# Hybrid decoder trunk on one core: the matmul queue's pair loop put at the start of a 16 KB piece of its program, two constant waits moved to their use, and the rotary keys' unit made fourth of the latent units

## The reference, cut to what matters

```python
def hybrid_layer(x, ...):
    h = rms_norm(x, norm_g)
    z = h @ w_in                     # 1024 x 9920, cut into eleven parts
    (x_rnn, g_rnn, sc_b, sc_c, x_sc, g_sc, c_q, c_kv, k_rope, g_att, gate_logits) = split(z)
    y_rnn = (rg_lru(x_rnn, ...) * silu(g_rnn)) @ rg_out
    y_sc  = (sc_b * depthwise(sc_c * x_sc) * silu(g_sc)) @ sc_out
    y_att = (mla(c_q, c_kv, k_rope, ...) * silu(g_att)) @ mla_out
    gates = sigmoid(gate_logits + gate_b)
    return x + (gates[0] * y_rnn + gates[1] * y_sc + gates[2] * y_att) @ w_out

def mla(c_q, c_kv, k_rope, ...):     # c_q 384 wide, c_kv 256, k_rope 64
    q = (rms_norm(c_q) @ w_uq)       # 8 heads of 128 + 64
    k = concat(rms_norm(c_kv) @ w_uk, k_rope for every head); v = rms_norm(c_kv) @ w_uv
    q, k = rms_norm(q), rms_norm(k); the last 64 of each are rotated by position
    return softmax(q k^T / sqrt(192), causal) @ v
```

## Time and profile before

| | us |
|---|---|
| median of 3 runs | 1804.34 (1803.9 to 1805.08) |
| the profiled execution's own time | 1801.34 |
| its span | 1799.5 |
| PE busy | 1742.7 (97%) |
| POOL, DVE, ACT busy | 1184.6, 807.1, 469.6 |

### The profile page before, as it was taken

How to read it: one execution, slowest core, us unless ns; L and a number is a source line. 1 busy time by engine, 2 the same in 40 slices (tenths; PEclk the granted TensorE clock), 3 DMA queues, 4 the chain that set the end, 5 groups by cost and what they waited for, 6 DMA issues and landing times.

```text
span 1799.5 us, 32868 instructions
## 1 busy us (share of the span) xinstructions
PE 1742.7 (97%) x12264; PEld 1634.6 (91%) x12264; DVE 807.1 (45%) x1373; ACT 469.6 (26%) x843; POOL 1184.6 (66%) x1365
## 2 busy tenths in 40 slices
PE   3998998989999999999999999999999999999999
PEld 3998998989999999999999899999998888888887
DVE  3764554436464453212246645555556544522121
ACT  3422323222233223101124323232322333311110
POOL 6474644536677886777775747465557888877773
PEclk9999999999999999999999999999999999999999
DMA  3322221212222323222342212212122222332233
GB/s 126 136 71 65 71 81 43 93 54 71 83 83 93 105 82 119 93 94 83 122 152 74 93 64 70 80 64 80 54 86 91 91 93 93 105 128 95 94 118 107
DMA packets 47515, 162.03 MB, mean 90 GB/s; under 512 B 5408, under 2 KB 6816, under 8 KB 47136
## 3 DMA queue, kind: packets, MB, share of 16 engines
q1 hardware_dynamic: 41328, 146.56, 25.0%
q10 hardware_dynamic: 6112, 14.39, 2.2%
HBM read 152.27 MB, written 10.81 MB: 91 GB/s over the span
## 4 chain that ended last, share of the span: by engine, by line
PE 95%; issue 1%; POOL 1%; DVE 1%; ACT 1%; DMA 0%; ACTq 0%; POOLq 0%; DVEq 0%
PE slots L507 83%; PE slots L565 4%; PE slots L598 2%; PE slots L657 2%; PE slots L541 2%; PE slots L583 1%; POOL early L467 1%; DMA residual_or_merged<-xt 0%; DVE spare L1116 0%; ACT early L911 0%; PE slots L568 0%; DVE branch_lo L1107 0%; PE slots L550 0%; ACT x_square L810 0%; DVE early L1160 0%
## 5 line engine op out<-in xcount | busy, mean ns | idle before, releaser
L419 POOL TENSOR_TENSOR w_lo<-w_raw,w_hi 128x256 fp32r<-128x256 f32 x1004 | 828.4, 856 | 20.9
L414 POOL TENSOR_SCALAR w_hi<-w_raw 128x1024 fp32r<-128x1024 f32 x251 | 284.9, 1135 | 412.9 <-PE slots L507 404.1
L507 PE MATMUL slots<-h_hi,w_hi 128*128 128x264 f32 (+1 forms) x2112 | 523.0, 312 | 0.0
L507 PE MATMUL slots<-h_lo,w_hi 128*128 128x264 f32 (+1 forms) x2112 | 516.5, 309 | 0.0
L507 PE MATMUL slots<-h_hi,w_lo 128*128 128x264 f32 (+1 forms) x2112 | 516.2, 309 | 0.0
L507 PEld LDWEIGHTS slots<-h_hi,w_hi 128*128 128x128 f32 x2112 | 344.0, 189 | 19.1
L507 PEld LDWEIGHTS slots<-h_hi,w_lo 128*128 128x128 f32 x2112 | 343.1, 189 | 19.1
L507 PEld LDWEIGHTS slots<-h_lo,w_hi 128*128 128x128 f32 x2112 | 343.0, 189 | 17.6
L507 PE MATMUL slots<-branch_hi,w_hi 128*128 128x264 f32 (+1 forms) x576 | 143.6, 313 | 27.9 <-ACT causal_r L830 27.9
L507 PE MATMUL slots<-branch_lo,w_hi 128*128 128x264 f32 (+1 forms) x576 | 142.8, 311 | 0.0
L507 PE MATMUL slots<-branch_hi,w_lo 128*128 128x264 f32 (+1 forms) x576 | 142.4, 311 | 0.0
(11 more groups left out here) (241 smaller groups left out, 2867.1 us busy)
## 6 DMA issues: line engine op xcount, KB each, us to landing
w_raw<-w_units SPq DMA_DIRECT2D x251, 512.0 KB, 3.3
stream<-sc_acc ACTq DMA_DIRECT2D x16, 264.0 KB, 3.1
sc_back<-stream SPq DMA_DIRECT2D x2, 2112.0 KB, 9.6
x_old<-stream SPq DMA_DIRECT2D x16, 264.0 KB, 4.3
stream<-residual_or_merged ACTq DMA_DIRECT2D x16, 264.0 KB, 2.1
ab_raw<-w_units SPq DMA_DIRECT2D x8, 512.0 KB, 4.1
residual_or_merged<-xt ACTq DMA_DIRECT2D x4, 528.0 KB, 7.9
stream<-xt ACTq DMA_DIRECT2D x1, 2112.0 KB, 10.7
```

The source lines that it names most:

```text
L414: pool.tensor_scalar(hi, raw, 1.0, 1.0, ALU.mult, ALU.mult).then_inc(sem("hi_part"), 1)
L419: op = pool.tensor_tensor(lo[:, cols], raw[:, cols], hi[:, cols].bitcast(F32), ALU.subtract)
L507: mm = pe.matmul(out[:, a_, 0:t1 - t0], w(k), x(k)[:, t0:t1], start=(n == 0), stop=(n == 3 * ks - 1))
```

## The change: what it does

Five edits.

1. The pair loop on PE gets `head_slot` 0: its first instruction is loaded at the start of a 16 KB piece. What lies between the code before it and that place is jumped over with at most one taken branch. It is done in both layers.
2. PE's three waits ahead of the layers go to their use, in layer 0 only: `made` before `stat`, `params_in` and `consts_ready` before `rot`.
3. `x_square` has four buffers in place of two (the first two of `h_tile` are added) and waits from the fifth block on, for the sum four blocks back.
4. The rotary keys' unit is fourth (kv0, kv1, q0, kr, q1, q2), in slot 0, and q1 goes into slot 2. On ACT kr's two instructions come before the root of `kv_ms` and the upper four blocks of h, and `q_latent(1)` after them. In layer 1 the wait for the stores moves with kr. On DVE `q_lower(1)` and `add_q_square(1)` go from behind the fourth block of h to behind the eighth.
5. `q_latent` squares first and makes the high part second; `add_q_square` has its own wait for the square, and for n = 2 it comes before `q_lower(2)`.

```diff
-    "CQ": [("kv0", 0, "unit_used"), ("kv1", 1, "unit_used"), ("q0", 2, "unit_used"), ("q1", 0, "unit_used"),
-           ("stat_kv", 1, "cq_mm"), ("kr", 2, "unit_used"), ("spread_kv", 1, "cq_mm"), ("q2", 0, "unit_used"),
+    "CQ": [("kv0", 0, "unit_used"), ("kv1", 1, "unit_used"), ("q0", 2, "unit_used"), ("kr", 0, "unit_used"),
+           ("stat_kv", 1, "cq_mm"), ("q1", 2, "unit_used"), ("spread_kv", 1, "cq_mm"), ("q2", 0, "unit_used"),
...
+            x_sq += h_tile[0:2]
...
-            pe.wait_ge(sem("made"), 5)
-            pe.wait_ge(sem("params_in"), 48)
-            pe.wait_ge(sem("consts_ready"), 2)
             for l in range(DEPTH):
...
                 latent("kv1", 1)
+                if l == 0:
+                    pe.wait_ge(sem("made"), 5)
                 out = free("NORM", l, 0, "stat")
...
-                latent("q1", 3)
+                latent("kr", 3)
...
-                latent("kr", 4)
+                latent("q1", 4)
...
                 out = free("CQ", l, 0, "rot")
+                if l == 0:
+                    pe.wait_ge(sem("params_in"), 48)
+                    pe.wait_ge(sem("consts_ready"), 2)
...
-                with pe.Fori(0, PAIRS) as p:
+                with nc.Fori(0, PAIRS, engines=bass.OrderedEngineSet([pe.engine]), head_slot={pe.engine: 0}) as p:
...
-                if c >= 2:
-                    act.wait_ge(*at("x_summed", l, 0, c - 1))
-                act.activation(x_sq[c % 2][:], xm[:, c, :], ACT.Square).then_inc(sem("x_squared"), 1)
+                if c >= 4:
+                    act.wait_ge(*at("x_summed", l, 0, max(1, c - 4)))
+                act.activation(x_sq[c % 4][:], xm[:, c, :], ACT.Square).then_inc(sem("x_squared"), 1)
...
+                    act.activation(halves(q_lat_sq[n][:]), src, ACT.Square).then_inc(sem("lat_squared"), 1)
                     act.activation(halves(cq_hi[:, n, :]), src, ACT.Identity, bias=zero,
                                    scale=hparam(l, CQ_G + n)).then_inc(sem("cq_hi"), 1)
-                    act.activation(halves(q_lat_sq[n][:]), src, ACT.Square).then_inc(sem("lat_squared"), 1)
...
-                q_lower(1)
-                add_q_square(1)
...
                 h_lower(7)
+                q_lower(1)
+                add_q_square(1)
...
+                add_q_square(2)
                 q_lower(2)
-                add_q_square(2)
```

More of the change, by code:

```diff
@@ L857, in _ @@
                     h_upper(k)
-                q_latent(1)
+                if l > 0:
+                    act.wait_ge(sem("stored"), l * (16 * KT))
+                act.wait_ge(*ready("CQ", l, 0, "kr"))
+                act.activation(halves(kr_gained[:]), slot(slot_of("CQ", "kr")), ACT.Identity, bias=zero,
+                               scale=hparam(l, KR_G)).then_inc(sem("kr_gained"), 1)
+                act.activation(halves(kr_sq), slot(slot_of("CQ", "kr")), ACT.Square).then_inc(freed("CQ", "kr"), 1)
                 act.wait_ge(*at("kv_ms", l, 0, 1))
@@ L864, in _ @@
                     h_upper(k)
-                if l > 0:
-                    act.wait_ge(sem("stored"), l * (16 * KT))
                 act.dma_start(xm[:, 0:2, :], rope).then_inc(sem("rope_in"), 16)
[L869 to L872, removed]
+                q_latent(1)
                 for n in range(KV):
@@ L1115, in x_sum @@
                     dve.wait_ge(*at("x_summed", l, 0, c - 1))
-                dve.tensor_tensor(spare[0][:], x_sq[0][:] if c == 1 else spare[0][:], x_sq[c % 2][:],
+                dve.tensor_tensor(spare[0][:], x_sq[0][:] if c == 1 else spare[0][:], x_sq[c % 4][:],
                                   ALU.add).then_inc(sem("x_summed"), 1)
@@ L1157, in add_q_square @@
                 def add_q_square(n):
+                    dve.wait_ge(*at("lat_squared", l, 0, KV + n + 1))
                     if n > 1:
@@ L1597 @@
         kr = w_in[:, K_ROPE:K_ROPE + ROPE]
-        units += [cols(w_in, C_KV, n) for n in range(KV)] + [cols(w_in, C_Q, n) for n in range(KQ - 1)]
-        units += [cols(np.concatenate([kr, kr], 1), 0, 0), cols(w_in, C_Q, KQ - 1)]
+        units += [cols(w_in, C_KV, n) for n in range(KV)] + [cols(w_in, C_Q, 0)]
+        units += [cols(np.concatenate([kr, kr], 1), 0, 0)] + [cols(w_in, C_Q, n) for n in range(1, KQ)]
         for p in range(PAIRS):
```

## The result

| | before | after |
|---|---|---|
| median, us | 1804.12 (1802.23 to 1805.08) | 1764.03 (1763.36 to 1765.3) |
| ratio, 95% interval | | 0.978 [0.9763, 0.9797] |
| the profiled execution's own time | 1801.34 | 1763.36 |

The change takes 40.1 us off. The page: span, busy time and instructions of the engines, then what PE's fetch queue q8 moved (packets, MB, its share); the earlier trace rows answers to the first two lines, and of q8 there were 57 packets.

A forecast was written before the change was run, and what follows sets the result against it. PE was taken to bound the kernel, busy 1742.7 of 1799.5 us. Gains of 17.5 + 2.3 + 22.4 = 42.2 us, off the median's 1804.3, gave 1762; own spread 1755 to 1768, range up to 1778.

The forecast's parts named there:

- its likeliest case: Whole kernel: the gains at the start, in the latents and at the loop's edges all come, 1762 us; chance 0.67.
- The start: Span's start to q0: without the early waits q0 begins at 25.5 instead of 43.04, 17.5 us less.
- The rival of the half-lost start: kv0 and kv1: PE works in fits, the clock stays low, gain only 12.3, time 1767; chance 0.09.
- The latent stage: Both layers' latents: the waits of stat_q for the second sum of squares go, 2.3 us less.
- The move of kr costs nothing: Latent stage: q1's slot is given back some 2 to 3 us before stat_kr needs it, so no loss.
- The pair loop: Layer 0's three back edges: 15.8 us of idle and 6.6 of slow matmuls go, 22.4 us less.
- The untested step: Pair loop on PE: the program store keeps 8 pieces, one fetched ahead, so the aligned body stays; no row shows it.
- The rival of one remaining fetch: Layer 0's edges: only 7 pieces stay, the head is missed, 9.3 us gained in place of 22.4, 1775; chance 0.13.
- the one of edges that stay: Layer 0's edges: head misplaced or nine pieces wanted, only 17.5 + 2.3 are left, 1784; chance 0.08.
- The clock dropped once without an edge: Pair loop turns: one fall at 1098, about 3.1 us of loss, counted the same once after, 3 us either way.
- The slower rival: Pair loop: jump and aligned head stop fetching ahead, 52 waits of 3.1 us, about 1945; chance 0.03.
- that jump: Ahead of each layer's pair loop: one branch over the filling, 0.2 us, while PE still has queued matmuls.

The follow-up runs named there:

- e4: The changed kernel without the pair loop's placement, its head three instructions ahead of the end of a piece: 1783.44 us, ratio 0.9888.
- e5: The changed kernel with the pair loop's head at slot 128 of a piece in place of 0: 1765.22 us, ratio 0.9793.
- e12: The changed kernel with eight unused matmuls in each turn's GpSimd wait and six more ahead of layer 0's first token sums: 1761.8 us, ratio 0.9782.
- e7: The changed kernel with two buffers for the squares again in place of four: 1770.7 us, ratio 0.9821.
- e9: The changed kernel with eight unused matmuls in each pair turn, where PE waits 0.91 us for GpSimd: 1754.06 us, ratio 0.9735.
- e3: The kernel before with only the new latent order: kr fourth, square ahead of high part, sum ahead of low part: 1800.58 us, ratio 0.9986.
- e2: The kernel before with only the early start: PE's three waits moved to their use, four square buffers: 1788.13 us, ratio 0.9913.
- e6: The changed kernel with the pair loop's head at slot 144, the body reaching ten instructions into an eighth piece: 1773.46 us, ratio 0.9841.
- e1: The kernel before with only the pair loop placed at the start of a 16 KB piece: 1785.94 us, ratio 0.9911.
- e8: The changed kernel with PE's three waits ahead of the layers again, four square buffers kept: 1773.4 us, ratio 0.9844.
- e10: The changed kernel with eight unused matmuls per pair turn ahead of the rotary queries' product, where PE doesn't wait: 1773.56 us, ratio 0.9846.
- e11: The changed kernel with four unused matmuls in each pair turn's GpSimd wait: 1755.43 us, ratio 0.9745.

## Why the prediction was right, and where its terms were off

The forecast was 1762 and the median is 1764.03; its range and its likeliest case held.

**The start, 17.5 forecast, 17.0 measured.** The steps came as written: first matmul at 8.85 (8.5), q0 at 26.05 (25.5), the sums in a row as what decides. The half microsecond lies on the path of the sums: they end at 24.85 instead of 24.7, the token sums start 0.14 us behind them, and take 1.06 us instead of 0.84. The later first branch_lo and 0.7 us of waiting for kv1's unit split cost nothing, as PE still waits 0.6 us for the last sum. In e4, e5 and e12 that split comes 0.8 to 1.0 us later, PE waits 1.9 us for it, and it decides in place of the sums (q0 at 27.7 in e5, where the clock fell as well). The clock, which the prediction named as a risk here, fell in the start in four of ten profiles with the early start (e4, e5, e7, e9). The rival of the half-lost start (q0 at 31) was not seen. e7 shows that edit 3 carries its share: without it q0 starts at 31.3.

**The latent stage, 2.3 forecast, 3.3 measured.** The wait ahead of `stat_q` went as counted, in e3 too. The stretch from q0 to the loop in layer 0 (columns as above), before and then after:

```profile
43.04:73.79 30.75, 29.51 (x236) 28.45 (x235) 24.88 (x47) 13.99 (x24) 12.33 (x14) 1.00 0.34 117
```

```profile
26.05:55.20 29.15, 29.15 (x235) 28.45 (x235) 26.32 (x46) 13.35 (x23) 18.96 (x22) 1.00 0.39 132
```

Of the 1.6 us, 1.24 were idle time, all of it gone, and 0.36 is PE's busy time for the same matmuls, which I hadn't counted. "The move of kr costs nothing" held in the sum, but for the order before only. It missed that with the early start DVE is late for `spread_kv` under the old order: e2 has a wait of 1.4 us there, and the change has none. Whether it is edit 4 or edit 5 that hides it wasn't run apart. The traces point to edit 4, since it takes q1's two operations on DVE from ahead of the diagonals: these are done 17.5 us behind q0's start in the change and 20.8 in e2.

**The pair loop, 22.4 forecast, 17.9 measured.** The mechanism is shown. The untested step, that 8 pieces stay, was taken on a guess ("the likelier size of a store") and holds: e5 (7 and one ahead) keeps them, e6 (8 and one ahead) doesn't, and e1 gets the edges' gain with edit 1 alone. The rival of one remaining fetch is out, as no branch of the change is above 0.4 us; so is the one of edges that stay, which e4 shows in its own kernel at 19.4 us. Four clean turns of 98.24 would be 393.0. Before, the 417.0 held 15.8 of idle time, 6.7 of slow matmuls behind the three edges (6.6 forecast), and 1.6 of something that the prediction overlooked: a fall of the clock for 3.4 us at 74.17, in the loop's first matmuls, which no edge precedes.

```profile
73.93 4.45 PE slots L657 x24
```

These take 4.45 us, and 2.94 in the change, which has no fall there. "The clock dropped once without an edge" was thus wrong by one. Why it fell is open: in the kernel before and in e1 it follows the wait of 1.14 us ahead of `stat_q`, but e4, e5 and e6 have a fall of 3.4 us at nearly the same place without such a wait. After, 399.2 holds 6.2 above clean, two falls of the clock of 3.1 us.

**The mis-sized term is the falls of the clock**: "I count it at the same once, and 3 us either way in the range". There were three, at 77, 374 and 1060. The two in layer 0 are new and make 6.2 us of the miss, beside 0.5 of the start and 0.2 of layer 1's loop; against them stand 1.7 of the loop's other rows and 1.0 of the latents, and 4.2 us are left. Over the change, e1 to e8 and e10, and the kernel before, the turns of eleven profiles had 24 falls in 88; all began 20.7 to 22.7 us into a turn, 1.8 to 2.9 us behind the end of the 0.91 us wait. Where the wait was filled or halved (e9, e11, e12) there were none in 24 turns. So more than one in a kernel was to be expected, and one profile of before couldn't show it. Why the clock falls in one such turn and not in the next stays open.

**The slower rival** (the jump stops the fetching ahead, 1945) did not occur in the loop: its pieces are crossed with no pause. e12 met something like it in one place and at 6.9 us. I had priced that jump at 0.2 us on the ground that PE still has queued matmuls; that holds in the change (0.3 us). With 12 instructions more ahead of it the same jump costs 6.4 us of idle PE, so that it was cheap here was luck that the prediction didn't name.

**The sum.** -17.0 - 3.3 - 17.9 + 0.2 is -38.0, which is what lies between the two profiled executions (1801.34 and 1763.36), where 42.2 was forecast. The medians differ by 40.1, as before's profiled execution was 2.8 us below its median and after's 0.7. The profiled sum was 4.2 us short, and the median came out only 2.0 us above the forecast because of this difference, which is luck.

## What to carry to other kernels

For a loop whose body is near the size of the fetched program's store, count the pieces that it touches plus one ahead, against 8 here: 16 instructions of placement decided 8 us, and slots 0 and 128 of a piece cost the same. When a wait goes, list what the earlier start lays on top of each other, and when code is added ahead of a placed loop, look at the branch that enters it. On an engine that bounds the kernel a wait of 0.9 us isn't worth 0.9 us but what the clock does behind it: with unused matmuls in it, the kernel that does more work is the faster.

## What the runs showed of the hardware that was not expected

- The store of PE's program behaves as one of 8 pieces of 16 KB, one of them fetched ahead: 7 and one stay (31 fetches, branches of 0.22 us), 8 and one don't (58 fetches, branches of 3.8 us).
- A missed head costs one pause (e6, 2.2 us of idle PE per edge) when it lies well inside its piece, and two (4.8 to 5.4 us) when the loop begins with the last two or three instructions of one, as before and in e2, e3 and e4.
- A branch from a piece over filling into another took 0.3 us in the change and 6.9 us in e12, with twelve more instructions ahead of it.
- The granted clock fell to the 1.2 GHz level for 6.7 to 6.8 us behind a 0.91 us wait between small matmuls in 24 of 88 turns, at 3.1 us each (101.33 against 98.23 in the change), and in none of 24 with four or eight more matmuls in the wait. With eight of the same elsewhere in the turn (e10) three of eight turns had a fall.
